# FFN waits on SiLU and root removed, opening's sum of squares shared between two engines, HGRN sample reads on four column tiles

## The reference, cut to what matters

```
for li in 0, 1:
    x += 0.5 * swiglu(rmsnorm(x))          # FFN: (silu(h @ wg) * (h @ wu)) @ wd
    x += mixer_li(rmsnorm(x))              # 0: HGRN2 || gated DeltaNet, 1: causal pooling
    x += 0.5 * swiglu(rmsnorm(x))
y = rmsnorm(x)
rmsnorm(x) = x * rsqrt(mean(x*x) + eps) * w
# HGRN2, one head, one sample token, S is 128 x 128:
S = diag(g) S + k v^T;   o = S^T q         # o = (diag(g) S)^T q + (k . q) v
```

## Time and profile before

| engine | busy us | share of the span |
|---|---|---|
| PE | 1042.4 | 97% |
| DVE | 679.2 | 63% |
| ACT | 513.1 | 48% |
| POOL | 88.7 | 8% |

### The profile page before, as it was taken

One profiled execution on the slowest core, in us unless ns is written; L12 is line 12 of the kernel. 1 busy time (PEld: TensorE's weight loads), 2 busy tenths in 40 slices (PEclk: granted clock), 3 DMA queues, 4 the chain that ended last, 5 costly groups with the idle time before them and its releaser, 6 DMA issues.

```text
span 1069.9 us, 21578 instructions
## 1 busy us (share of the span) xinstructions
PE 1042.4 (97%) x8482; PEld 1024.5 (96%) x8482; DVE 679.2 (63%) x875; ACT 513.1 (48%) x689; POOL 88.7 (8%) x152
## 2 busy tenths in 40 slices
PE   8999999999999998999999999999999999999998
PEld 7999999989898987999999999999999989999997
DVE  5666654478968556866665467666545986666543
ACT  6444443465683544644444364444434464444434
POOL 5800000010001110200000020000001020000001
PEclk9899999999999999999999999999999999999999
DMA  7565655789794422566655558566555436665551
GB/s 221 160 203 177 187 167 189 134 206 185 154 140 156 116 73 67 168 203 181 178 177 178 178 159 250 178 176 177 178 182 171 138 111 200 182 179 177 178 176 41
DMA packets 135062, 177.92 MB, mean 166 GB/s; under 512 B 5806, under 2 KB 120574, under 8 KB 134992
## 3 DMA queue, kind: packets, MB, share of 16 engines
q1 hardware_dynamic: 131600, 165.74, 54.8%
q0 software_dynamic: 3328, 11.38, 3.6%
q10 hardware_dynamic: 80, 0.05, 0.0%
HBM read 171.19 MB, written 6.52 MB: 166 GB/s over the span
## 4 chain that ended last, share of the span: by engine, by line
PE 87%; DVE 7%; ACT 3%; issue 1%; DMA 1%; ACTq 0%; DVEq 0%
PE ps L1547 26%; PE ps L1548 26%; PE ps L1549 26%; PE ps L1373 1%; DVE w_lo L1062 1%; PE ps L1380 1%; ACT w_hi L518 1%; DVE C L648 1%; DMA raw<-in_w_in_even 1%; DVE xw_lo L1083 1%; PE ps L1362 1%; DVE rstd L1089 1%; PE ps L1392 1%; PE ps L1535 0%; DVE x L1071 0%
## 5 line engine op out<-in xcount | busy, mean ns | idle before, releaser
L1062 DVE TENSOR_TENSOR w_lo<-raw,w_hi 128x1024 fp32r<-128x1024 f32 x311 | 381.6, 1229 | 298.5 <-ACT w_hi L518 297.7
L518 ACT CAST w_hi<-raw 128x1024 fp32r<-128x1024 f32 x311 | 324.5, 1049 | 440.7 <-PE ps L1549 417.3
L1547 PE MATMUL ps<-xw_hi,w_hi 128*128 128x264 f32 x1472 | 422.8, 287 | 7.0 <-ACT sg L548 4.6
L1548 PE MATMUL ps<-xw_lo,w_hi 128*128 128x264 f32 x1472 | 421.7, 286 | 0.0
L1549 PE MATMUL ps<-xw_hi,w_lo 128*128 128x264 f32 x1472 | 420.9, 286 | 0.0
L1547 PEld LDWEIGHTS ps<-xw_hi,w_hi 128*128 128x128 f32 x1472 | 279.7, 190 | 10.4 <-issue 7.7
L1549 PEld LDWEIGHTS ps<-xw_hi,w_lo 128*128 128x128 f32 x1472 | 278.9, 189 | 0.0
L1548 PEld LDWEIGHTS ps<-xw_lo,w_hi 128*128 128x128 f32 x1472 | 278.6, 189 | 0.1
L1549 PE MATMUL ps<-a_hi,w_lo 128*128 (+1 forms) x704 | 200.6, 285 | 0.0
L1547 PE MATMUL ps<-a_hi,w_hi 128*128 (+1 forms) x704 | 200.4, 285 | 0.0
L1548 PE MATMUL ps<-a_lo,w_hi 128*128 (+1 forms) x704 | 200.3, 285 | 0.0
(11 more groups left out here) (350 smaller groups left out, 792.9 us busy)
## 6 DMA issues: line engine op xcount, KB each, us to landing
raw<-in_ffn_w_gate SPq DMA_DIRECT2D x88, 512.0 KB, 3.8
raw<-in_ffn_w_up SPq DMA_DIRECT2D x88, 512.0 KB, 3.8
raw<-in_ffn_w_down SPq DMA_DIRECT2D x88, 512.0 KB, 3.4
raw<-in_w_in_even SPq DMA_DIRECT2D x32, 512.0 KB, 7.7
raw<-in_w_out_even SPq DMA_DIRECT2D x8, 512.0 KB, 4.2
raw<-in_pool_w_in SPq DMA_DIRECT2D x8, 512.0 KB, 3.5
out<-SBUFS POOLq DMA_DIRECT2D x4, 512.0 KB, 3.8
PT<-in_x_prompt SPq DMA_DIRECT2D x2, 512.0 KB, 4.3
```

Of the source, the lines that this page charges most:

```text
L518: nc.scalar.copy(w_hi[:, w % SPL, :], raw[:, w % RAW, :]).then_inc(hi_done, 1)
L1062: nc.vector.tensor_tensor(w_lo[:, w % SPL, :], raw[:, w % RAW, :], w_hi[:, w % SPL, :].bitcast(F32), ALU.subtract).then_inc(lo_done, 1)
L1547: mm(out, wh, hi, start=first, stop=False)
L1548: mm(out, wh, lo, start=False, stop=False)
```

## The change

Four edits:

1. PE's waits for `silu_done` ahead of each block and for `root_done` ahead of block 1 are removed.
2. In the first FFN, `tick(s + 2)` moves ahead of the root on ACT and ahead of the reciprocal on DVE; `norm(0)` moves ahead of slot 3 on PE.
3. For norm 0, POOL adds 5 squares rather than 8, and PE sums the other 3 by itself.
4. HGRN's reads become two groups (head pairs y = 0 and 1) in rounds 3 and 6, in the form of the DeltaNet reads: DVE writes padded query columns (HQ4), PE runs 16 matmuls on four column tiles, ACT copies the rows, PE transposes in rounds 4 and 7, DVE takes the columns; PE waits for the last of these ahead of the product in bank 6.

```diff
-POOLED = (8, 7, 8, 8, 7, 8, 7)
+POOLED = (5, 7, 8, 8, 7, 8, 7)
...
+        HQ4 = KTf[:, 768:896].rearrange("p (y z bh bl m) -> p y z bh bl m", y=2, z=2, bh=2, bl=4)
+        HREADS = (KTf[:, 896:1024], KTf[:, 0:128])
...
+            def read_rows(y):
+                act.wait_ge(st("samp_read"), y + 2)
+                A.copy(HREADS[y], ps[:, 6, 128 * y:128 * y + 128]).then_inc(st("read_rows"), 1)
...  (ACT: read_rows(1) behind gates[1] in l = 6, read_rows(0) at the end of l = 3)
                     tick(s + 1, i)
+                    tick(s + 2, i)
                     if b == 0:
                         root(FFN_NORM[n])
-                    tick(s + 2, i)
                     silu(b, i)
...
+            dve.wait_ge(st("qk_zero"), 2)
+            hq = SMALL[:, 224:256].rearrange("p (y z bh bl) -> p y z bh bl", y=2, z=2, bh=2)
+            for z in range(2):
+                for bh in range(2):
+                    ins = V.tensor_copy(HQ4[:, :, z, bh, :, 2 * z + bh], hq[:, :, z, bh, :])
+            ins.then_inc(st("qk4"), 1)
...
+            def read_columns(y):
+                dve.wait_ge(st("read_T"), y + 2)
+                V.tensor_copy(rdh[:, y].rearrange("p z bh bl -> p (z bh) bl"),
+                              ps[:, 6, 256 + 128 * y:384 + 128 * y].rearrange("p (bl m) -> p m bl", bl=4)[:, 0:4, :])\
+                    .then_inc(st("qk4"), 1)
...
+                if r == 5:
+                    read_columns(0)
+            read_columns(1)
...
-            dve.wait_ge(st("samp_read"), 5)
+            dve.wait_ge(st("qk4"), 4)
...
                     else:
+                        if n == 0:
+                            tick(s + 2)
                         root_inverse(FFN_NORM[n])
                     gate(b, i)
-                    tick(s + 2, i)
+                    if b:
+                        tick(s + 2, i)
...
+                if r in (4, 7):
+                    y = r // 7
+                    pe.wait_ge(st("read_rows"), y + 2)
+                    tr(ps[:, 6, 256 + y * P:256 + (y + 1) * P], HREADS[y], ident[:, :]).then_inc(st("read_T"), 1)
...
-                if r - 1 in READ:
-                    j = READ[r - 1]
-                    pe.wait_ge(st("samp_dec"), j + 1)
-                    for b in range(NSAMP):
-                        c = 8 * (j - 4) + b
-                        ins = mm(ps[:, 7, c:c + 1], SV(j)[:, b, :], SMALL[:, 224 + c:225 + c], start=True, stop=True)
+                if r in (3, 6):
+                    y = r // 6
+                    pe.wait_ge(st("samp_dec"), 6 + 2 * y)
+                    pe.wait_ge(st("qk4"), 2 + y)
+                    for z in range(2):
+                        for bh in range(2):
+                            for bl in range(4):
+                                ins = mm(ps[32 * bl:32 * bl + 4, 6, y * P:(y + 1) * P], HQ4[:, y, z, bh, bl, :],
+                                         SV(4 + 2 * y + z)[:, 4 * bh + bl, :], start=z + bh == 0, stop=z + bh == 2)
                     ins.then_inc(st("samp_read"), 1)
...
+            pe.wait_ge(st("qk4"), 4)
             for h in range(4):
                 ins = mm(psB[:, h, :], U[:, h, :], VT[:, h, :], start=True, stop=True)
...
-                alone = POOLED[n] < KD
-                if alone:
-                    pe.wait_ge(sq_done, 8 * n + KD)
-                    mm(ps[:, sum_bank(n), 0:TOK], mean_w[:, :], hn[:, KD - 1, :], start=True, stop=False)
+                alone = range(POOLED[n], KD)
+                for z in alone:
+                    pe.wait_ge(sq_done, 8 * n + z + 1)
+                    mm(ps[:, sum_bank(n), 0:TOK], mean_w[:, :], hn[:, tile_of(n, z), :], start=z == alone[0], stop=False)
...
                 xw_slot(2, 0, banks + 2)
+                norm(0)
                 xw_slot(3, 1, banks + 2)
-                norm(0)
...
-                    if b:
-                        pe.wait_ge(silu_done, v(b, i, 2))
...
-                pe.wait_ge(root_done, nn + 1)
...
+            G.memset(KTf[:, 768:896], 0.0).then_inc(st("qk_zero"), 1)
```

More of the change, by code:

```diff
@@ L440, in even_scalar @@
                     gates[1]()
+                    read_rows(1)
                     act.wait_ge(st("gates"), 1)
@@ L450, in even_scalar @@
                     A.copy(U[:, :, :], psC).then_inc(st("inv"), 1)
+                if l == 3:
+                    read_rows(0)
             act.wait_ge(st("tiles_T"), 5)
@@ L837, in even_vector @@
             V.tensor_scalar(QP, QP, DH ** -0.5, None, ALU.mult).then_inc(st("hg_q"), 1)
+            dve.wait_ge(st("qk_zero"), 2)
[4 more added lines that the diff above has]
+            ins.then_inc(st("qk4"), 1)
+            rdh = SMALL[:, 256:288].rearrange("p (y z bh bl) -> p y z bh bl", y=2, z=2, bh=2)
+            def read_columns(y):
[3 more added lines that the diff above has]
+                    .then_inc(st("qk4"), 1)
             slots(30, 31)
@@ L936, in even_vector @@
             V.tensor_tensor(O[:, 4:8, smp], hb(rdq), hb(WV[:, 2, :]), ALU.add).then_inc(st("so"), 1)
-            V.tensor_tensor(O[:, 0:4, smp], hb(ps[:, 7, 0:32]), hb(WV[:, 4, :]), ALU.add).then_inc(st("so"), 1)
+            V.tensor_tensor(O[:, 0:4, smp], hb(SMALL[:, 256:288]), hb(WV[:, 4, :]), ALU.add).then_inc(st("so"), 1)
             totc = tots[-1].rearrange("p (h c) -> p h c", h=4)[:, :, 1:2].broadcast_to([P, 4, P])
```

## The result

| | median us | lowest to highest | executions |
|---|---|---|---|
| before, same chip | 1073.32 | 1070.66 to 1077.2 | 4 |
| after | 1063.73 | 1062.26 to 1064.8 | 4 |

The ratio is 0.9911, 95% interval 0.9892 to 0.993: faster by 9.6 us. Forecast were 1061.3 us and a gain of 11.1. The profiled execution of after took 1064.8 us (span 1063.1, mean clock 0.998), 6.9 less than that of before.

The account below looks back on a forecast made before the run. PE was taken to bound the kernel, with 87% of the chain of waits. Opening 5.85, other FFNs 1.8 and reads 3.45 sum to 11.1 us; 1072.46 less this is 1061.4, taken as 1061.3, range 1058 to 1066.5.

Parts of the forecast that it names:

- The opening: First FFN up to slot 6: PE runs on without the 3.9 us stall and the low clock behind it, 5.85 us gained.
- the thin margin: Norm 0 in the first FFN: POOL's four adds end at 20.7, 0.3 us before PE comes to the sum.
- the term of 2.75: Behind the opening's stall: 27 matmuls at full clock take 3.25 us rather than 6.0, 2.75 us gained.
- The rule on the shared port: Opening's root chain: VectorE and GpSimd lock each other out, so POOL's masks could cost five DVE steps up to 0.6 us each.
- The other FFNs: Block 1 of FFNs 1 to 3: the small PE stalls go with the removed waits, 1.8 us gained, bounds 1.2 to 2.2.
- The reads: HGRN reads in the mixer rounds: two groups of 32 passes replace four of 16, 3.45 us gained, bounds 1.5 to 4.8.
- The 0.2 charged for DVE's four copies: Ahead of slot 30: DVE's four copies make the evacuation PE waits for 0.1 to 0.3 late, costing 0.2 us.
- One of the prediction's signs of being wrong: Mixer: a wait of PE for `qk4` or the row copy that is over 0.2 us.
- fourth rival: Mixer rounds: more waiting makes the clock fall, slower; all of it low would cost 35 us, 1096; chance 0.03.
- 1, the stall at slot 6: Opening: the stall moves to the product wait at slot 6, giving back 1 to 3 us, 1064.4; chance 0.13.
- 2, a mixer bound by DVE: Mixer: DVE binds every round, so the reads were hidden anyway; only 7.65 us gained, 1064.8; chance 0.12.
- 3, no effect in the FFNs: FFNs: a wait for split weights holds PE at slots 4 and 5, leaving only the mixer's 3.45, 1069; chance 0.03.

Follow-up runs that it names:

- e4: The kernel before, run again unaltered: 1072.12 us, ratio 0.999 to before.
- e2: The kernel before with only the HGRN reads changed to two groups on four column tiles: 1068.79 us, ratio 0.9958 to before.
- e12: The kernel before with the loads of DeltaNet states 0 and 1 moved from the projection into the first FFN: 1069.03 us, ratio 0.9956 to before.
- e1: The kernel before with the removed waits, new opening order and shared sum, HGRN reads as before: 1066.18 us, ratio 0.9931 to before.
- e3: The changed kernel, run again unaltered: 1063.73 us, ratio 0.9909 to before.
- e8: The changed kernel with nine unused matmuls filling PE's idle ahead of the output projection: 1061.74 us, ratio 0.9895 to before.
- e10: The changed kernel with POOL adding all 8 squares of norm 0 again: 1066.07 us, ratio 0.9927 to before.
- e11: The changed kernel with HGRN's first read group split over rounds 3 and 4, its transpose in round 5: 1062.18 us, ratio 0.9887 to before.
- e5: The kernel before with only PE's waits for SiLU and root removed: 1067.04 us, ratio 0.9943 to before.
- e6: The kernel before with only the new opening order and the shared sum, both PE waits kept: 1067.45 us, ratio 0.9947 to before.
- e7: The changed kernel with the loads of DeltaNet states 0 and 1 moved from the projection into the first FFN: 1059.70 us, ratio 0.9881 to before.

## Why the prediction was right, and what it lacked

**The opening was right: 5.85 forecast, 5.93 in the pair of traces.** The root started 0.64 after the last sum (0.75 forecast), the product was 2.0 us early (1.7), the clock stayed. POOL's four adds took 3.77 us, not the 4.6 that the mean of seven gave, so the thin margin did not matter. One size held for the one execution only: the low stretch behind the stall had 27 matmuls there, but (counted as those of 0.30 us and more) 28 in e4, 18 in e2 and 13 in e12, which have the same stall of 3.9 us. The old opening took 208.58, 208.74, 207.49 and 207.26 us, 208.0 on average; the new one 202.65 to 202.67 in all seven profiles that have it. So the mean gain is 5.4, and the term of 2.75 was 0.6 too large as an average.

**The rule on the shared port did not decide.** Two readings of the prediction were off here. POOL's masks did not move to beside the root chain: they stood beside it already (POOL busy for 3.47 of the 3.80 us from 25.00 before, 3.40 after). And the root chain has little that the rule bears on. DVE's reciprocal took 1.80 and its gate 0.71, as in all other places; the Trainium skill (SBUF — State Buffer, "SBUF: two separate sides") holds back DVE only in its two-port modes or, against a GpSimd operation that reads SBUF, with two SBUF inputs, and the reciprocal has one input, the gate's second is in PSUM. Two rows do fit the rule: of the three splits, which have two SBUF inputs, the one beside POOL's last add took 1.66, the two beside the masks 1.30 each, where 1.23 is the mean; and POOL's mask step at 28.41, begun while DVE's factor ran (28.19 to 28.90), took 1.00 and ended 0.5 behind it, where the same step took 0.65 at 26.72. DVE, having started first, lost nothing.

**The other FFNs: 1.8 forecast, 1.82 measured** (0.42, 1.0 and 0.42 forecast by stage; 0.38, 0.99 and 0.45 measured). The other blocks gave nothing, as forecast.

**The reads: 3.45 forecast, 3.32 measured,** and 3.3 in all six profiles that have edit 4 in its own form. Round 2 gave 1.67 (1.65); round 3 0.55 (0.8), since a group of 32 takes 0.99 with a further 0.1 at the change of tile form, where 0.9 was taken from the DeltaNet row; round 4 -0.11 (-0.1); round 5 1.28 (1.3); rounds 6 and 7 -0.1 to 0 (0). The 0.2 charged for DVE's four copies was not paid: from the Gram product to the rounds both traces have 39.56 us. One of the prediction's signs of being wrong did show, without cost: the product behind the loop that waits for `qk4` starts 1.21 us after the transpose ahead of it, where it stood 0.93, 0.28 later, but the next product's wait of 0.26 for ACT is gone in turn.

**What failed is the scope of the sum.** "Together 5.85" was carried through the projection as if that stage were paced by PE alone. PE is busy for most of it (55.61 of the 57.00 us from 205 before), but its weights take 7.8 us a piece by the page, those of the FFNs' gate and up products 3.8, and where one is late PE stands. Its length went from 61.80 to 64.70 us in this pair. The sum had a term of 0 there without naming what hid it. Over the runs, the six profiles with edits 1 to 3 and late states lie at 62.32 to 66.66 (after, e1, e3, e8, e10 with its changed form, e11; mean 64.0), the five with less of the change (before, e2, e4, e5, e6) at 61.80 to 62.66 (mean 62.0).

Part of the 2.0 us between the means is clock: behind an idle in the projection the matmuls ran at the lower level in e1 (15 of them), e3 (11), e8 (13) and e11 (15), which at 0.10 each is 1.1 to 1.5 us, or 0.9 in the mean of the six; in after, e10 and the five others they did not. e8, and then e3:

```profile
251.81 0.59 PE L1587 MATMUL ps<-x_hi,w_hi 128*128 128x264 f32 x1 [2.04 <-DVE PT L666]
252.00:255.00 3.00, 3.00 (x14) 3.00 (x15) 2.56 (x5) 0.84 (x1) 0.00 (x0) 0.50 1.00 266
```

```profile
269.84 0.59 PE L1585 MATMUL ps<-x_hi,w_hi 128*128 128x264 f32 x1 [3.55 <-DVE PT L666]
```

The prediction looked for a falling clock only in the rounds (its fourth rival), and the projection is where the change came with one.

By averages the terms are 5.4 + 1.8 + 3.3 - 2.0 = 8.5 us; the medians say 9.6 and, for the same program in e3's series, 9.0, with an uncertainty of about 2. They would bear a sum without the -2.0 as well, 10.5, so that this term rests on the profiles.

**What stays open** is why the projection is longer with edits 1 to 3 together, or whether it is. A shifted start alone does not do it: e5, whose lead at norm 1 is 4.3 us, has 61.88, and e6 61.82. Among the six, the length goes with ACT's waits for the weights: 15.9 us in e10 (62.32), 19.0 in e11 (62.43), 19.3 in e8 (62.82), 21.0 in after (64.70), 21.1 in e1 (65.12), 22.4 in e3 (66.66). e7 and e12 show that without the two state loads the stage is short in either form; what makes the transfers later in some executions than in others is not shown. Chance has a large part: after, e3, e8 and e11 have the same code up to the end of this stage, and lie between 62.43 and 66.66.

**The rivals.** 1, the stall at slot 6: refuted, the product is 2.0 us early. 2, a mixer bound by DVE: refuted by rounds 2, 3 and 5. 3, no effect in the FFNs: refuted by 5.93 and 1.82. 4, the clock falling in the mixer's rounds: refuted, from round 2 on no idle of PE in the rounds is over 0.61 us, and the window from 333 to 391 us shows a clock of 1.00 with PE busy for 54.99 of 58.00.

## What to carry to other kernels

Where a stall is removed, ask of the next stage what paces it; if that is transfers, an earlier start is no gain until they too are counted, and loads that can go elsewhere should. A stall of PE is worth its own length and the low-clock stretch behind it. Here either of two edits that brought an idle of 3.9 us to 1.0 or 1.35 took most of both, so that the two did not add. A term taken from a low-clock stretch of one execution should carry a spread: here 13 to 28 matmuls behind the same stall. And a term taken from one pair of traces should be measured again in a second pair: the projection, 2.9 us longer in the first, lay anywhere from 0.6 to 4.9 above before's 61.80 in others with the same code up to there.

## What the runs showed of the hardware

- The granted clock fell from 1.00 to 0.50 or 0.51 behind idles of PE of 3.91 and 3.96 us in the opening, 2.44 ahead of the output projection and 3.55 in the projection (e3), and did not behind 1.35 and 1.00 (e5, e6) at the same place in the opening. Between these it went either way, in the projection: it fell within about a microsecond of the end of idles of 2.04 (e8), 1.84 (e1) and 1.76 us (e11), and not behind 2.04 (e3), 2.03 (e1), 2.01 (after), 1.92 (e5) and 1.90 (e2). So the length of the idle alone did not decide.
- A one-column float32 read with a 128x128 stationary operand took 106 ns a pass (1.70 us for 16), one with 4 stationary columns and 128 moving ones about 31 (0.99 for 32).
- From 250 to 254 us, in the projection, the DMA engines moved 83 to 89 GB/s at a share of 0.94 and 0.95, from 25.00 to 28.80 us, in the first FFN, 308 GB/s at 0.93: a full DMA share says nothing of the bandwidth. That the slow rate is not the state loads' doing shows in e12, 103 GB/s from 240 to 254 us with no packet of theirs.
- An operation of DVE with two SBUF inputs (a split) took 1.66 us where POOL was adding when it began, 1.30 beside POOL's masks, 1.23 in the mean; a mask step of POOL that began during DVE's factor took 1.00 rather than 0.65.
